# Sample gate in two column halves, state update on four row groups of 32 tokens, the first tile's output projection begun behind the prompt's scan, and more of its expert choice inside the sample scan

## Time and profile before

| | us |
|---|---|
| median of 3 runs | 2562.1 |
| lowest, highest | 2558.26, 2571.83 |
| the profiled execution, its own time | 2563.79 |
| its span in the trace | 2562.0 |
| TensorE busy (70%) | 1794.2 |
| VectorE busy (61%) | 1575.0 |
| GpSimd busy (52%) | 1324.9 |
| ScalarE busy (12%) | 305.0 |
| DMA | 859 MB, mean 335 GB/s |

### The profile page before, as it was taken

The page is one execution under the profiler, slowest core; times in us unless marked ns, Lnnn a source line. Parts: engine busy times, 40 slices in busy tenths (PEclk is TensorE's granted clock), DMA queues, the critical chain, the costliest instruction groups (busy, mean ns, idle before and its releaser), DMA issues.

```text
span 2562.0 us, 23629 instructions
## 1 busy us (share of the span) xinstructions
PE 1794.2 (70%) x7688; PEld 800.3 (31%) x7688; DVE 1575.0 (61%) x3823; ACT 305.0 (12%) x705; POOL 1324.9 (52%) x1480
## 2 busy tenths in 40 slices
PE   7999888676405666668778576776665658456678
PEld 4477756524400010022334223351123422001112
DVE  2288875999798656652644988768764353833321
ACT  2133322201000000010101011110012110000000
POOL 0011443255547777755665445754555363577774
PEclk9999899887756666788899786787777778699999
DMA  4232228599989999999999999999999999999997
GB/s 154 99 104 95 90 80 282 165 357 386 403 293 388 409 409 409 409 395 402 384 407 401 402 401 358 407 400 400 399 374 349 320 378 374 388 409 410 409 408 305
DMA packets 325848, 859.13 MB, mean 335 GB/s; under 512 B 26841, under 2 KB 93353, under 8 KB 325697
## 3 DMA queue, kind: packets, MB, share of 16 engines
q0 software_dynamic: 184320, 671.17, 66.7%
q1 hardware_dynamic: 141406, 186.46, 21.0%
HBM read 845.25 MB, written 12.17 MB: 335 GB/s over the span
## 4 chain that ended last, share of the span: by engine, by line
DMA 23%; POOL 18%; PE 12%; issue 8%; DVE 5%; SPq 3%; ACT 0%; POOLq 0%; DVEq 0%; ACTq 0%
POOL arena L2564 18%; DMA arena<-peer_v,arena 10%; DMA wring<-w_q 5%; PE banks L896 4%; PE banks L1103 3%; DMA wring<-cache_v 2%; DVE arena L2220 2%; DMA arena<-peer_u,arena 2%; SPq L1336 2%; DMA wring<-w_kv 1%; PE banks L1012 1%; SPq L1334 1%; DMA wring<-ple_w_gate 1%; DMA wring<-peer_w_query 1%; PE banks L560 1%
## 5 line engine op out<-in xcount | busy, mean ns | idle before, releaser
L2220 DVE SCALAR_TENSOR_TENSOR arena<-arena,banks 128x1024 f32<-128x1024 f32 x640 | 762.3, 1219 | 441.5 <-DMA arena<-peer_u,arena 435.7
L1103 PE MATMUL banks<-arena 128*32 128x512 f32 x2560 | 692.9, 718 | 351.6 <-DMA arena<-peer_v,arena 344.6
L2564 POOL DMA_INDIRECT arena<-peer_v,arena x640 | 607.8, 950 | 416.7 <-PE banks L1103 179.8
L2564 POOL DMA_INDIRECT arena<-peer_u,arena x640 | 606.8, 948 | 412.3 <-issue 188.7
L1103 PEld LDWEIGHTS banks<-arena 128*32 128x32 f32 x2560 | 92.5, 116 | 823.5 <-DMA arena<-peer_v,arena 655.2
L896 PE MATMUL banks<-wring,uT 128*128 128x512 f32 (+3 forms) x448 | 224.2, 650 | 67.5 <-DMA wring<-w_q 28.0
L560 PE MATMUL banks<-cst,arena 128*128 128x128 f32 (+6 forms) x498 | 78.0, 305 | 163.1 <-DVE arena L2236 83.4
L896 PEld LDWEIGHTS banks<-wring,uT 128*128 128x128 f32 (+1 forms) x448 | 80.2, 189 | 219.0 <-issue 168.1
L630 PE MATMUL banks<-uT,wring 128*128 128x320 f32 x512 | 139.1, 433 | 0.0
L560 PEld LDWEIGHTS banks<-cst,arena 128*128 128x128 f32 (+6 forms) x498 | 60.5, 156 | 213.8 <-DVE arena L2236 83.6
L588 PE MATMUL banks<-wring,uT 128*128 128x512 f32 (+1 forms) x256 | 115.8, 609 | 0.6 <-DVE arena L2103 0.6
(11 more groups left out here) (265 smaller groups left out, 1941.6 us busy)
## 6 DMA issues: line engine op xcount, KB each, us to landing
wring<-peer_w_query SPq DMA_DIRECT2D x40, 1024.0 KB, 17.1
wring<-ssm_w_in SPq DMA_DIRECT2D x24, 1024.0 KB, 7.3
wring<-w_q SPq DMA_DIRECT2D x18, 1024.0 KB, 21.0
wring<-ssm_w_out SPq DMA_DIRECT2D x16, 1024.0 KB, 9.3
wring<-ple_w_gate SPq DMA_DIRECT2D x12, 1024.0 KB, 12.6
arena<-peer_u,arena POOLq DMA_INDIRECT x640, 12.0
arena<-peer_v,arena POOLq DMA_INDIRECT x640, 12.4
out_sample_ssm<-arena SPq DMA_DIRECT2D x16, 512.0 KB, 5.6
```

The costliest lines, as they stand in the source:

```text
L1103: mm = pe.matmul(sums(t, at, half), place_of(t, at), rows_buf[:, k, half * 512:(half + 1) * 512], start=at < spots(t), stop=False, skip_gr ...
L2220: dve.scalar_tensor_tensor(rows_buf[:, k, :], rows_buf[:, k, :], 1.0, u_now, ALU.mult, ALU.mult, accum_out=pact[:, n % 2, at:at + 1]).then ...
L2564: pool.indirect_dma_start(rows_buf[:, k, :], None, tables[kind], bass.IndirectOffsetOnAxis(ap=rows, axis=0))\
```

## The change

- The gate's weights go through `gate_block`: the sample tile's 512 columns are two products of 256 columns, one into partitions 0 to 63 and one into 64 to 127 of the bank. ScalarE and VectorE read the two halves one by one.
- The state update takes the 32 partitions from 64i + 32q for head pair i and token half q; tokens 32q to 32q + 31 are four sequences. The pattern is a new constant of 4 columns.
- The first tile's output projection: block 0 stands behind the last step of the prompt's scan, block 1 in sample group 0. The four quarters of its weights, and those of the other tiles' projection, free their slots one by one (`part_read`). Its loads are issued ahead of the prompt's last two state stores.
- Norm, queries and scores of the first tile stand one group earlier. The expert choice begins in group 3 with 3, 3, 2, 2 and 2 steps, and may go on into quad 2; `first_select` has two steps less.

```diff
--- before.py
+++ after.py
@@ -34,10 +34,10 @@
 NB = 8
 NW = 4
 
-ARENA = 31744
-
-
-C_ID, C_TRI, C_STRICT, C_TRIS, C_STRICTS, C_ONES, C_BM, C_ID2, C_IOTA, C_END = 0, 128, 256, 384, 448, 512, 640, 648, 712, 728
+ARENA = 31736
+
+
+C_ID, C_TRI, C_STRICT, C_TRIS, C_STRICTS, C_ONES, C_BM, C_ID2, C_IOTA, C_SEQ, C_END = 0, 128, 256, 384, 448, 512, 640, 648, 712, 728, 736
 
 
 def shape_constants():
@@ -53,7 +53,7 @@
     c[:64, C_STRICTS:C_STRICTS + 64] = (k > s) & same
     c[:, C_ONES:C_ONES + 128] = 1.0
     c[:64, C_BM:C_BM + 8] = k // DEC_T == np.arange(8)[None, :]
-    c[64:, C_BM:C_BM + 4] = k // DEC_T == 4 + np.arange(4)[None, :]
+    c[:, C_SEQ:C_SEQ + 4] = np.arange(128)[:, None] // DEC_T % 4 == np.arange(4)[None, :]
     c[:, C_ID2:C_ID2 + 64] = np.arange(128)[:, None] % 64 == np.arange(64)[None, :]
     c[:, C_IOTA:C_IOTA + 16] = np.arange(16)[None, :]
     return c
@@ -258,13 +258,18 @@
             pe.wait_ge(w_ready[i % NW].sem, 16 * (i // NW + 1))
             return slot_view(i)
 
+        part_read = signal("weight_part_read")
         load_sent = [0]
 
         def load_weights(sp, upto):
             while load_sent[0] < upto:
                 i = load_sent[0]
                 if i >= NW:
-                    sp.wait_ge(*full_at(last_user[i - NW]))
+                    user = last_user[i - NW]
+                    if user is not None and user[0] == "read":
+                        sp.wait_ge(*part_read.at(user))
+                    else:
+                        sp.wait_ge(*full_at(user))
                 sp.dma_start(slot_view(i), loads[i][0]).then_inc(*w_ready[i % NW].mark(by=16))
                 load_sent[0] += 1
 
@@ -590,9 +595,20 @@
                         if kk == kchunks - 1:
                             mm.then_inc(*full((key, n, t)))
 
-            def project(key, nblocks, kchunks):
-                for n in range(nblocks):
-                    project_block(key, n, kchunks)
+            def gate_block(n):
+
+                acc = {t: claim(pe, ("z", n, t)) for t in ALL}
+                for half in range(2):
+                    w = weight(pe, ("z", n, half), ("z", n, 2))
+                    for t in ALL:
+                        for k in range(4):
+                            kk = half * 4 + k
+                            for c in range(1 if t < 2 else 2):
+                                out, cols = (acc[t], w[:, k, :]) if t < 2 else \
+                                    (acc[t][64 * c:64 * c + 64, 0:256], w[:, k, 256 * c:256 * c + 256])
+                                mm = pe.matmul(out, uT[:, kk, OFF[t]:OFF[t] + ROWS[t]], cols, start=(kk == 0), stop=(kk == KD - 1))
+                        if half == 1:
+                            mm.then_inc(*full(("z", n, t)))
 
             pe.wait_ge(*cst_in.at("cst"))
             norm_transposes("mix0")
@@ -604,7 +620,7 @@
                         mm = pe.matmul(acc[rows, 0:32], uT[:, k, OFF[t]:OFF[t] + ROWS[t]], w_dt[:, k, :],
                                        start=(k == 0), stop=(k == KD - 1))
                 mm.then_inc(*full(("dt", t)))
-            project_block("z", 0, KD)
+            gate_block(0)
 
             pe.wait_ge(rows_in.sem, 64)
             for half in range(2):
@@ -612,7 +628,7 @@
                                             for j in range(16)])
             transposes("ng", [(0, ng_rows)])
             for n in range(1, 4):
-                project_block("z", n, KD)
+                gate_block(n)
 
             def to_tokens(n):
 
@@ -662,7 +678,7 @@
                 pe.wait_ge(*dve_done.at(("bm", g)))
                 for i in range(2):
                     for q in range(2):
-                        rows = slice(64 * q, 64 * q + 64)
+                        rows = slice(64 * i + 32 * q, 64 * i + 32 * q + 32)
                         bank = claim(pe, ("hupd", 2 * g + i, q))
                         mm = pe.matmul(bank[:, :], xdtt[rows, x, i * 128:(i + 1) * 128],
                                        bm[rows, g % 2, :, :], start=True, stop=True)
@@ -752,21 +768,29 @@
                     pe.wait_ge(*freed(("q", b)))
                 scores(0, 0, [q])
 
+            def out_block(n):
+
+                bank = claim(pe, ("out", n, 0))
+                for part in range(4):
+                    pe.wait_ge(*freed(("yT", 0, part)))
+                    w = weight(pe, ("out", n, part), ("out", n, 0) if part == 3 else ("read", "out", n, part))
+                    for k in range(4):
+                        kk = part * 4 + k
+                        mm = pe.matmul(bank, uT[:, kk, 0:128], w[:, k, :], start=(kk == 0), stop=(kk == 15))
+                    mm.then_inc(*(full(("out", n, 0)) if part == 3 else part_read.mark(("read", "out", n, part))))
+
             def after_sample_turn(g):
 
                 if g == 0:
                     turn_sub_keys(0)
-                    for q in range(4):
-                        pe.wait_ge(*freed(("yT", 0, q)))
-                if g < 2:
-                    project_block("out", g, 16, (0,))
-                if g == 2:
+                    out_block(1)
+                if g == 1:
                     pe.wait_ge(*freed(("sk", 0)))
                     norm_transposes("ffn0", (0,))
-                if 2 <= g < 6:
-                    first_queries(g - 2)
-                if g in (3, 4, 6):
-                    first_scores((0, 1, None, 2)[g - 3])
+                if 1 <= g < 5:
+                    first_queries(g - 1)
+                if g in (2, 3, 5):
+                    first_scores((0, 1, None, 2)[g - 2])
 
             for q in range(6):
                 for t in range(3):
@@ -796,6 +820,8 @@
                 scan_back(*divmod(n, GROUPS))
                 if n % GROUPS == 0 and n > 0:
                     turn_rows(n // GROUPS - 1)
+                if n == 2 * GROUPS - 1:
+                    out_block(0)
                 if n >= 2 * GROUPS:
                     after_sample_turn(n - 2 * GROUPS)
             turn_rows(2)
@@ -1124,7 +1150,7 @@
                 for n in range(2):
                     acc = {t: claim(pe, ("late_out", n, t)) for t in (1, 2)}
                     for part in range(4):
-                        w = weight(pe, ("late_out", n, part), ("late_out", n, 2))
+                        w = weight(pe, ("late_out", n, part), ("late_out", n, 2) if part == 3 else ("read", "late_out", n, part))
                         for t in (1, 2):
                             for k in range(4):
                                 kk = part * 4 + k
@@ -1132,6 +1158,8 @@
                                                start=(kk == 0), stop=(kk == 15))
                             if part == 3:
                                 mm.then_inc(*full(("late_out", n, t)))
+                            elif t == 2:
+                                mm.then_inc(*part_read.mark(("read", "late_out", n, part)))
                         yield
                     yield
                 yield
@@ -1157,7 +1185,7 @@
             second_select = select(0, 1)
 
             def first_select():
-                for _ in range(10):
+                for _ in range(8):
                     yield
                 yield from finish_select(0, 0)
 
@@ -1280,6 +1308,7 @@
             sp.wait_ge(*full_at(("state", 1, 7)))
             load_state(2)
             load_state(3)
+            load_weights(sp, load_index[("out", 0, 0)] + 8)
             for g in (6, 7):
                 store_final(g)
             for g in range(8):
@@ -1287,8 +1316,8 @@
                     if blk + 4 < 16:
                         load_state(blk + 4)
                     store_state(blk)
-                if g < 6:
-                    load_weights(sp, load_index[("out", 0, 0)] + (8, 10, 14, 16, 18, 20)[g])
+                if g < 5:
+                    load_weights(sp, load_index[("out", 0, 0)] + 12 + 2 * g)
 
             def store_tokens(t):
                 sp.wait_ge(*dve_done.at(("ple", 1, 1, t)))
@@ -1429,8 +1458,12 @@
             for n in range(4):
                 for t in range(3):
                     bank = filled(act, ("z", n, t))
-                    s(act.activation(z[0:ROWS[t], t, n * 512:(n + 1) * 512], bank[0:ROWS[t], :], ACT.Tanh, scale=0.5),
-                      act_done, ("ztanh", n, t))
+                    if t < 2:
+                        s(act.activation(z[:, t, n * 512:(n + 1) * 512], bank, ACT.Tanh, scale=0.5), act_done, ("ztanh", n, t))
+                    else:
+                        for c in range(2):
+                            s(act.activation(z[0:64, 2, n * 512 + 256 * c:n * 512 + 256 * c + 256],
+                                             bank[64 * c:64 * c + 64, 0:256], ACT.Tanh, scale=0.5), act_done, ("ztanh", n, 2))
                 if n == 0:
                     for half in range(2):
                         bank = filled(act, ("rows", half))
@@ -1502,16 +1535,15 @@
 
                 if g == 0:
                     take_sub_keys(0)
```

(35 more changed lines are left out.)

## The result

The changed kernel takes 2504.49 us (median of 4 runs, 2501.63 to 2508.55) against 2566.97 us (4 runs, 2558.26 to 2572.65) for the kernel before in the same comparison: ratio 0.9761, 95% interval 0.9725 to 0.9797. The profiled execution took 2501.63 us, with a span of 2499.8.

What follows compares the result with a forecast made beforehand. A front of engines waiting for each other, then 2050 us of gathers bound by transfers; 2563.8 - 13.65 (gate) - 7.0 (scan) - 1.5 (phase 0) = 2541.6, forecast 2540 us against the median, range 2530 to 2553.

Steps and rivals of the forecast that it cites:

- The gate, 13.65: Sample tile's gate: 32 products of 512 columns become 64 of 256 in overlapping pairs, 13.65 us less.
- (d): Gate: pairs of 256 columns don't overlap, loads stay hidden; no gain in the gate, 2553.5 us; chance 0.04.
- (e): Gate: weight loads are exposed, so the gate loses 17.9 us; kernel slower at 2571.5 us; chance 0.03.
- Row groups, 0.85 per group: Sample scan's state update: four row groups save 0.85 us per group; at 0, some 2.5 us of the sum lost.
- The scan, 7.0: Sample scan: turned rows start at 506.2 in place of 513.2, 7.0 us less; bounds 15 less and 0.
- rival (a): Sample scan: GpSimd slows VectorE's extra choice steps and the 7 us goes; 2548.5 us; chance 0.17.
- Phase 0, 1.5: Phase 0's gathers: VectorE has two search steps less, 5 us; 1.5 counted since transfers are mostly full.
- rival (b): Phase 0 keeps all its relief, 5 us, and the scan gives 12, beside the gate's 13.65; 2531 us; chance 0.12.
- rival (c): Behind the scan: the stretch at 740 to 760 us lengthens, half of 22 us is left; 2551 us; chance 0.06.

## Why the prediction was wrong

The step that failed is the one that took the transfers as given: "afterwards it reads 9 in nearly every slice", a half "bound by transfers" at 405 GB/s, for which I counted only "1.5" in phase 0 and nothing else behind the scan. The change's smallest line, eight more columns of constants, stood in the diff and I never priced it. Alone it gives 61.6 and 45.9 us in two comparisons, and the unused tile in its place 62.0. None of the rivals had it, so no chance was on the cause that decided, and the range was built without it. In the changed kernel the same step of placement is worth 52.9 us (2555.6, the mean of the two slow placements, to 2502.7, the mean of the two fast ones).

The schedule at a slow placement gave 13.6 to 16.6 us, where its sum was 22.1. At a fast one the only runs beside each other give 9.4 us (2510.18 to 2500.82, two executions each). Term by term:

- **The gate, 13.65: right.** Its blocks go from 21.28 to 17.88 us, 3.40 each and 13.6 in all. The x/B/C products start 15.1 us earlier (117.83 to 102.71). The other 1.5 lie mostly ahead of the gate's first block, which the gate doesn't touch: it starts at 27.97 us before and at 26.76 after, within the 25.7 to 28.3 between which it starts in the other traces. Rivals (d) and (e) fall: the busy time of the group halved with twice the loads. The rule of the Trainium skill ("TensorE: Matmul & The Clock Gate", Part 3, The mechanism), by which loads overlap only where the row group differs, is not borne out by these pairs either.
- **Row groups, 0.85 per group: right in size (1.99 to 1.14), nearly worthless in place.** It moved the first gather by 0.4 us (0.1 from the gate's start), below even the "some 2.5 us" at stake in the sum.
- **The scan, 7.0: too much; 2.7 were measured** (497.91 to 495.16, the row groups among them; 2.4 to 2.5 from the gate's start). The part that I summed from rows held: 63.2 us from the choice's beginning to the scaling, 63.7 measured. The start of that chain was off. With the measured 15.1 us of the gate in place of 13.65, the second block should have ended at 370.2 and the choice begun at 417.7; they came at 374.4 and 421.27, 4.2 and 3.6 us late. The delay arises on TensorE between the blocks: I named the wait for the bank of block 0, but took VectorE to be through with it 1.5 us sooner (350.8 against 352.26), and the products behind it at 1.97 us, their time at full clock. They took 3.52, at a granted clock of 0.57. In the kernel before they took 3.68 us at 0.50, so the block that now stands in front of them did not keep the clock up. The other 1.2 us are spread over that group's small pieces. Of the 7.0, 3.6 went there and 0.5 in the choice's own chain. Most of the 7 us went, as rival (a) had it, but hardly by its mechanism, for that chain held.
- **Phase 0, 1.5 (bounds 0 and 5): about 2 at the slow placement (1.7 to 2.5), 4 to 7 at the fast one.** That would fit transfers that bind less, so that VectorE's relief counts more, as in rival (b)'s half; no run separates it.
- **What arrives.** At the start of phase 4 the changed kernel at a slow placement is 18 to 24 us ahead of the one before (1716.4 and 1713.3 against 1734.3 and 1737.1), and at the fast placement 23 (1682.2 against 1705.5, means of two and three executions), close to the 22.1 forecast. In phase 4 it loses 10 to 13 us of it again at the slow placement, in two traces against two. That is rival (c), a part of the shift lost behind the scan, in size if not in place: I had it at 740 to 760 us, and gave it 0.06. By the end of phase 0 the lead had grown, from 16.5 us at the first gather to 18.9. At the fast placement the loss lies between 1 and 15 us and can't be told from phase 4's scatter.

## What to carry to other kernels

In a stretch bound by transfers, first ask where their targets lie: a constant that grows by eight columns moves every later buffer, and here that was worth three to four times the schedule work in the same change. Compare schedules only at equal placement, and try an unused tile of 32 to 224 bytes ahead of the DMA buffers before any reordering (here 32 bytes were right, and 64 and 160 were not). Price short products from the row of the very step that will run there, with its clock, and not from the same instruction one step on.

## What the runs showed of the hardware

- The start of the target rows in SBUF changes the rate of full DMA engines from 409 to 420 GB/s at the same busy share (1.03), and a 4 KB row from 163.1 to 159.0 ns: of shifts by 0, 32, 64, 160 and 288 bytes only 32 and 288 are fast.
- In all five traces of the new order TensorE stands idle for 3.87 us ahead of group 0's products with old states, and these take 3.35 to 3.68 us, where 1.97 is their time at a granted clock of 1.00. In the changed kernel the clock in that window is 0.57.
- Products of 32 rows on four row groups: eight records in 1.14 us, where two row groups needed 1.99, both at full clock.
- VectorE's 128x512 product takes 0.69 us alone, but 2.27 in one place where GpSimd ran 128x1024 ones (440.63 to 445.28 us). The changed kernel's timeline of VectorE:

```profile
441.26 2.27 DVE L2100 TENSOR_TENSOR arena<-arena 128x512 f32<-128x512 f32 x1
...
475.45 0.69 DVE L2100 TENSOR_TENSOR arena<-arena 128x512 f32<-128x512 f32 x1
```
